# Delta units that cross between halves of the array, attention heads in pairs, layers written out

## The chip, the cores and the metric

The kernel runs on one core of a Trainium2 chip. The core has TensorE (PE, matrix products from SBUF into PSUM), VectorE (DVE), ScalarE (ACT), GpSimd (POOL) and SyncE (SP, which issues most transfers), each with its own in-order queue of instructions, coupled by semaphores. The metric is the device time of one execution in microseconds; lower is better. The profile and all its rows come from one profiled execution.

## What is computed

The reference has two parts that follow each other on one sequence of 256 tokens with 1,024 channels, in f32. Cut to what this change touches:

```python
def first_block(x, c, ctx, ...):             # one layer
    z_x, z_c = split(norm(x) @ w_in), split(norm(ctx) @ w_in)
    ya = rwkv_mixer(z_c, z_x, ...)           # 8 heads of 64, both directions, 512 tokens
    yb = na_mixer(z_c, z_x, ...)             # 8 heads of 64, 256 queries, 512 keys
    x = x + gate * branch_merge(ya, yb)
    return x + gate * moe(norm(x))

# rwkv_mixer, one step of the scan, per head and direction (s is 64x64):
s = s * w_t - (s @ kk_t) (kk_t * a_t)^T + v_t k_t^T ;  y = s @ r_t

# na_mixer, per head:
q = rms_norm(q) * q_g * 64 ** -0.5 ; k = rms_norm(k) * k_g
p = softmax([q @ k_x^T + bias (masked to a window), q @ k_c^T]) ; y = p @ [v_x; v_c]

# second part: two layers (each: four mixers, merge, then 8 heads x 16 looked-up experts a token)
for l in range(2):
    x = layer(x, weights[l])
```

## The kernel before

`build` runs `first_block` and then `second_block`. Every stage is a block of its own that ends with a barrier of all engines, and no work is begun across one.

`first_block`: the input products (`linear`), `head_scales` (the norms of the heads, which also multiplies q by the gain `q_g`), `na_attention`, `delta`, `close`, `moe`. `second_block` (L3485) is a loop on the chip, `Fori(0, 2)`, over `layer`, which runs `mixers` and `merge_peer`; the layer's number is a register, from which SP computes the addresses of the weights. In `merge_peer` each token's 128 experts are gathered row by row.

`na_attention` (L1376) works on units, a head and one half of the queries (128 queries x 512 keys, of which the first 256 are context), 16 in all. Per unit: PE multiplies scores (L1416; a head's 64 channels lie on one half of the partitions), DVE scales the context half (L1468), scales the other half and adds the masked bias (L1470), takes the maximum of 512 columns (L1473) and negates it (L1474), ACT takes the exponential and the sum (L1450), DVE the reciprocal (L1486) and the division of all 512 columns (L1487), PE transposes (L1439), ACT copies (L1459), PE mixes with v into 64 output rows (L146), DVE copies out (L1480). PE's order puts the scores of unit n+2 ahead of the transposes of unit n. GpSimd adds the mask to the bias (L1406).

`delta` (L561) does the scan in 4 steps of 128 tokens, both directions (d) at once, by chunks of 64 tokens: 16 units of a head and a direction, each with two chunks, one on either half of the partitions (`half(c)`). A triangular system is inverted by squaring: the matrix P and its transpose lie in `MP[:, u, 0:2]`, the sum so far in `MP[:, u, 2]`. In round s of 0 to 5 (`SQ` is 5) PE squares P (L739), multiplies the transpose and, from round 1, the sum (L743, L746), for 8 groups of two units; ACT copies the powers back (L889, 128x256, 128x128 in round 4), DVE adds the product to the sum (L1029, 128x128), after ACT. All products here go from half c to half c, so two of the four 64x64 quadrants of PE are in use, in turn. Behind round 0 PE has the products with V (L696) and the turning of tokens (L711), which waits for DVE's tails (L982, L983), behind round 1 the decays' logs of the next step (L644). DVE has the tails, the blends of the next step (L934 to L939), then the sums, and behind rounds 2 and 3 the operands of the next step (L950 to L965). ACT copies the turned tokens between rounds 0 and 1 (L903 to L906), and behind round 1 the exponentials of the next step (L871). After round 5 come the solution (L763), the factor (L771: the one product here whose four quadrants alternate, two of them into each bank), the state's additions and its advance. The other order of things is set by the code as written, engine by engine.

## Time and profile before

| | us |
|---|---|
| median of 3 runs | 2974.51 (2971.76 to 2982.3) |
| the profiled execution: its time | 2983.61 |
| its span, first to last instruction | 2981.8 |
| `na_attention` (238.8 to 291.7) | 52.9 |
| `delta` (292.2 to 553.1) | 260.9 |
| layer 0 of `second_block` (1035.6 to 2004.1) | 968.5 |
| layer 1 (2004.2 to 2976.9) | 972.7 |

A row of the timeline has the start, the duration, the engine, the line, the operation, output and inputs, the partitions x columns and the count; in brackets stands the idle time before it and who ended it. "issue" is idle time that nothing in the profile explains. PE's products in f32 stand in the trace as two instructions each, its transposes as one; L644's 8 products of a step, for instance, are x16. PEld is the load of weights. A window's row has the busy time of PE, PEld, DVE, ACT and POOL with their counts, then PEclk, the granted clock of PE as a share of 2.4 GHz (0.5 is its lower level, 1.2 GHz), and the transfers' share and rate.

### The profile page before, as it was taken

Reading aid. Unit: us, or ns where it says so; the run is one execution under the profiler, and the core shown is the slowest. Engines: PE = TensorE matmul, PEld = TensorE weight load, DVE = VectorE, ACT = ScalarE, POOL = GpSimd, SP = SyncE. Lnnn points to the kernel's source line nnn. Section 1 sums busy time; section 2 is a strip of 40 time slices with the busy share of each in tenths; the row PEclk is TensorE's granted clock in tenths of the full one; section 3 lists DMA queues with packets and bytes.
Section 4 is the critical chain, followed back from the end, with each engine's and each line's share of the span. In section 5 each row is a group of like instructions: output and inputs, shape, how many; then the busy total and the mean of one; then the engine's idle time right before and its main releaser. Section 6 shows DMA issues by size and latency. Waiting matters only on the chain. (4 is left out here: it accounts for less than half of the span.)

```text
span 2981.8 us, 44173 instructions
## 1 busy us (share of the span) xinstructions
PE 2631.6 (88%) x17318; PEld 1869.5 (63%) x17318; DVE 1994.0 (67%) x4159; ACT 1177.4 (39%) x2270; POOL 656.9 (22%) x570
## 2 busy tenths in 40 slices
PE   7999888889999799999997787879999999887877
PEld 5895788778888689985553333338998555333333
DVE  5546665559999656567767777645665777677764
ACT  4243554348888544522222222234552322213222
POOL 0001000000004100004444454420000444454442
PEclk9999999989999899999999999989999999899998
DMA  7640000339999443359999999974345999999997
GB/s 311 235 187 24 3 3 3 121 127 351 371 379 371 166 161 128 142 200 417 421 417 422 422 421 421 421 315 163 117 152 198 395 421 418 422 421 421 421 422 320
DMA packets 121060, 838.88 MB, mean 281 GB/s; under 512 B 15402, under 2 KB 18380, under 8 KB 19732
## 3 DMA queue, kind: packets, MB, share of 16 engines
q0 software_dynamic: 77600, 564.43, 45.8%
q1 hardware_dynamic: 43252, 271.59, 24.2%
q8 instruction: 141, 2.31, 0.3%
q14 instruction: 67, 0.55, 0.1%
HBM read 834.65 MB, written 1.05 MB: 280 GB/s over the span
## 5 line engine op out<-in xcount | busy, mean ns | idle before, releaser
L3087 PE MATMUL bank<-uv_rows,z_o 128*128 128x512 f32 x872 | 435.1, 645 | 85.1 <-ACT z_o L3215 85.0
L3087 PEld LDWEIGHTS bank<-uv_rows,z_o 128*128 128x128 f32 x872 | 176.0, 206 | 320.1 <-issue 209.5
L3430 DVE CUSTOM_DVE_ANT_0 uv_rows<-uv_rows,ring 128x1024 f32<-128x1024 f32 x218 | 265.6, 1224 | 162.6 <-DMA uv_rows<-in_peer_uv,peer_index 162.2
L2967 POOL DMA_INDIRECT uv_rows<-in_peer_uv,peer_index x218 | 251.8, 1155 | 411.5 <-PE bank L3087 253.4
L3087 PE MATMUL bank<-z_mg,z_o 128*128 128x512 f32 x528 | 259.9, 638 | 55.4 <-ACT z_o L3215 55.3
L1805 DVE TENSOR_TENSOR moe_halves<-ring,moe_halves 128x1024 fp32r<-128x1024 f32 x240 | 285.6, 1221 | 29.7 <-ACT moe_halves L1729 27.4
L3087 PE MATMUL bank<-query_weights,z_o 128*128 128x512 f32 x544 | 256.7, 619 | 55.1 <-ACT z_o L3215 55.1
L3209 ACT ACTIVATE peer_gelu<-peer_act 128x4 f32<-128x4 f32 (+2 forms) x134 | 27.5, 205 | 703.2 <-DVE peer_act L3430 703.2
L3215 ACT ACTIVATE z_o<-square,peer_wts 128x128 f32<-128x128 f32 x512 | 164.4, 390 | 257.1 <-DVE peer_wts L3444 240.1
L1729 ACT ACTIVATE moe_halves<-ring 128x1024 fp32r<-128x1024 f32 x240 | 249.0, 1059 | 42.7 <-PE bank L161 42.4
L2630 DVE TENSOR_TENSOR x_weights<-ring,x_weights 128x1024 fp32r<-128x1024 f32 x116 | 140.7, 1224 | 156.9 <-ACT x_weights L2470 156.4
L159 PE MATMUL bank<-x_halves,x_weights 128*128 128x256 f32 x800 | 233.5, 292 | 2.5 <-DVE x_nk L2639 2.5
L3430 DVE CUSTOM_DVE_ANT_0 query_weights<-query_weights,ring 128x1024 f32<-128x1024 f32 x136 | 165.2, 1225 | 93.1 <-DMA query_weights<-in_peer_uv,peer_index 93.1
L3087 PEld LDWEIGHTS bank<-query_weights,z_o 128*128 128x128 f32 x544 | 104.1, 196 | 196.2 <-issue 119.9
L3087 PEld LDWEIGHTS bank<-z_mg,z_o 128*128 128x128 f32 x528 | 105.3, 205 | 193.1 <-issue 122.5
L160 PE MATMUL bank<-x_halves,x_weights 128*128 128x256 f32 x800 | 226.3, 283 | 0.0
L161 PE MATMUL bank<-x_halves,x_weights 128*128 128x256 f32 x800 | 226.1, 283 | 0.0
L3430 DVE CUSTOM_DVE_ANT_0 z_mg<-z_mg,ring 128x1024 f32<-128x1024 f32 x132 | 160.8, 1224 | 91.4 <-DMA z_mg<-in_peer_uv,peer_index 91.4
L2967 POOL DMA_INDIRECT z_mg<-in_peer_uv,peer_index x132 | 158.9, 1203 | 190.0 <-PE bank L3087 174.6
L2967 POOL DMA_INDIRECT query_weights<-in_peer_uv,peer_index x136 | 157.0, 1154 | 158.0 <-PE bank L3087 141.8
L2470 ACT ACTIVATE x_weights<-ring 128x1024 fp32r<-128x1024 f32 x116 | 121.9, 1056 | 174.6 <-PE bank L161 174.6
L159 PEld LDWEIGHTS bank<-x_halves,x_weights 128*128 128x128 f32 x800 | 153.1, 191 | 10.0 <-issue 6.3
(644 smaller groups left out, 5729.6 us busy)
## 6 DMA issues: line engine op xcount, KB each, us to landing
ring<-in_moe SPq DMA_DIRECT2D x96, 1024.0 KB, 6.9
ring<-in_w_in SPq DMA_DIRECT2D x83, 1024.0 KB, 5.0
ring<-in_mod_rows SPq DMA_DIRECT2D x16, 1024.0 KB, 4.8
ring<-in_w_out SPq DMA_DIRECT2D x12, 1024.0 KB, 6.8
ring<-in_mod_w SPq DMA_DIRECT2D x8, 1024.0 KB, 11.9
ring<-in_w_branch SPq DMA_DIRECT2D x8, 1024.0 KB, 8.8
query_weights<-in_peer_wq SPq DMA_DIRECT2D x8, 1024.0 KB, 9.9
ring<-in_peer_wq SPq DMA_DIRECT2D x6, 1024.0 KB, 6.5
```

Source lines behind the costliest of these rows:

```text
L159: pe.matmul(out, a[0], b[0], start=first, stop=False)
L160: pe.matmul(out, a[0], b[1], start=False, stop=False)
L161: return pe.matmul(out, a[1], b[0], start=False, stop=last)
L1729: act.activation(w2[:, p % 4, 0, :], C.ring[:, n % RING, COLUMNS[c]], ACT.Copy)\
L1805: dve.tensor_tensor(w2[:, p % 4, 1, :], C.ring[:, n % RING, COLUMNS[c]], w2[:, p % 4, 0, :].bitcast(F32), ALU.subtract).then_inc(S["low"], 1)
L2470: act.activation(w2[:, p % 4, 0, :], C.ring[:, n % TS, COLUMNS[c]], ACT.Copy).then_inc(S["high"], 1)
L2630: dve.tensor_tensor(w2[:, p % 4, 1, :], C.ring[:, n % TS, COLUMNS[c]], w2[:, p % 4, 0, :].bitcast(F32), ALU.subtract).then_inc(S["low"], 1)
L2967: pool.indirect_dma_start(out=row(j), out_offset=None, in_=A["peer_uv"], in_offset=bass.IndirectOffsetOnAxis(ap=index[:, g, k:k + 1], axis ...
L3087: ins = pe.matmul(bank[2 * t + c][:, :], diag[:, q % 2, i, :], row(j)[:, D + c * 512:D + (c + 1) * 512], start=(j % (PH * TOPK) == 0), sto ...
L3209: act.activation(gel[:, q % 2, 0:size], acts[:, g % 2, c:c + size], ACT.Gelu).then_inc(S["gelu"], 1)
L3215: ins = act.activation(diag[:, q % 2, n, :], C.sq["ident"], ACT.Copy, scale=wts[:, q % 2, n:n + 1])
L3430: dve.tensor_tensor_reduce(u, u, xtok[:, t, :], 1.0, 0.0, ALU.mult, ALU.add, acts[:, g % 2, j % TOPK:j % TOPK + 1]).then_inc(S["dots"], 1)
```

## The change

In `delta`, a unit's place changes from round to round: `lies(i, s, c)` tells on which half chunk c of unit i lies in round s. The first unit of a pair stays on its half; the second goes over to the other half in rounds 1, 2, 3 and 4, there and back, so that the products of rounds 1 to 4 use all four quadrants; rounds 0 and 5 use two. The products are issued for two groups at a time (`square_round`), as 64x64 products, by kind, then by unit, then by chunk; a bank holds the first or the second units of two groups (a batch). The sum is written otherwise: `MP` has four parts, P, its transpose, P plus the identity (2) and the product so far (3). DVE no longer adds to the sum in SBUF: `advance_sums` writes, out of PSUM and with a mask of identity and zero, parts 2 and 3 in one addition (128x256; in rounds 0 and 4 only part 2, 128x128; in round 5 a copy). Round 0 now has such additions too. ACT takes the batches in the order 0, 1, 2, DVE in the order 1, 0, 3, 2, each waiting so that they are not in the same bank. From round 2 on eight banks are used in place of four. `MP` is larger, `ZT` moves into `ya`.

In `na_attention`, a pair is two heads, one on either half of the partitions. The scaling by 64 ** -0.5 goes into `q_g` in `head_scales`. The bias has a context half of zeros, cleared by GpSimd; one `tensor_tensor_reduce` adds it and takes the maximum of 512 columns. The division goes: DVE makes a diagonal of reciprocals, and PE multiplies with it where it transposed (a product, so two instructions for one). The mixes of the two heads alternate between halves of the output rows. Scores of pair m+2 now stand behind the turning of pair m.

In `second_block` the loop is a Python loop: the layers stand one behind the other in the program, with fixed addresses.

```diff
+                dve.tensor_scalar(C.v["q_g"], C.v["q_g"], HD ** -0.5, None, ALU.mult).then_inc(S["q_gain"], 1)
...
+    rbank = lambda s, b: bank[b % 4 if s < 2 else b]
+    batch = lambda b: slice(2 * groups[b - b % 2][1] + groups[b][0] * NH + b % 2,
+                            2 * groups[b - b % 2][1] + groups[b][0] * NH + b % 2 + 3, 2)
+    def lies(i, s, c):
+        return c ^ (i & (s - 1) & 1) if s else c
...
+                def emptied(s, b):
+                    if s < 2 and b >= 4:
+                        taken(s, b - 4)
+                    elif s == 1 or s == 2 and b < 4:
+                        taken(s - 1, b + 4)
+                    elif s == 2:
+                        pe.wait_ge(S["tok"], len(turns))
+                        pe.wait_ge(S["w_out"], 2)
+                        if not last:
+                            pe.wait_ge(stages[step + 1]["decays"], 4)
+                def square_round(s, k):
+                    powers = ([(1, 0, 0)] if s < SQ else []) + ([(0, 1, 1)] if s < SQ - 1 else []) + \
+                             ([(2, 3, 2)] if s else [])
+                    for q in range(2):
+                        for left, right, at in powers:
+                            for i in range(2):
+                                u = groups[2 * k + q][0] * NH + 2 * groups[2 * k + q][1] + i
+                                out = rbank(s, 2 * k + i)[:, q * 192 + at * CH:q * 192 + (at + 1) * CH]
+                                for c in range(CC):
+                                    h, to = half(lies(i, s, c)), half(lies(i, min(s + 1, SQ), c))
+                                    part = lambda n: X[h, u, 0, :] if s == 0 and n == 1 else MP[h, u, n, :]
+                                    ins = pe.matmul(out[to], part(left), part(right), start=True, stop=True)
+                    ins.then_inc(S["round"], 1)
                 for s in range(SQ + 1):
-                    for g, (d, p) in enumerate(groups):
...
-                                    ins = pe.matmul(out[r, 2 * CH:3 * CH], m, MP[r, u, 2, :], start=True, stop=True)
-                        ins.then_inc(S["round"], 1)
+                            taken(s - 1, 2 * k + 1)
+                        emptied(s, 2 * k + 1)
+                        square_round(s, k)
...
+                    to, of = (slice(0, 2), slice(0, 2)) if s < SQ - 1 else (slice(3, 4), slice(2, 3))
+                    for b in range(NG):
+                        act.wait_ge(S["round"], s * (NG // 2) + b // 2 + 1)
+                        if b % 2:
+                            act.wait_ge(S["summed"], s * NG + b)
+                        act.activation(MP[:, batch(b), to, :], rbank(s, b)[:, 0:384]
+                                       .rearrange("p (u a t) -> p u a t", u=2, a=3)[:, :, of, :], ACT.Copy)\
+                           .then_inc(S["power"], 1)
                     if s == 1 and not last:
                         decays(step + 1)
                     if s == 0:
...
                                       units(X, d)[:, :, 0, :], ALU.subtract).then_inc(S["start"], 1)
+                def advance_sums(s, b):
+                    dve.wait_ge(S["round"], s * (NG // 2) + b // 2 + 1)
+                    if s < SQ and b % 2 == 0:
+                        dve.wait_ge(S["power"], s * NG + b + 1)
+                    of = rbank(s, b)[:, 0:384].rearrange("p (u a t) -> p u a t", u=2, a=3)
+                    if s == SQ:
+                        ins = dve.tensor_copy(MP[:, batch(b), 3, :], of[:, :, 2, :])
+                    elif s in (0, SQ - 1):
+                        ins = dve.tensor_tensor(MP[:, batch(b), 2, :], of[:, :, 0, :],
+                                                C.masks[:, 4, :].unsqueeze(1).broadcast_to([P, 2, CH]), ALU.add)
+                    else:
+                        ins = dve.tensor_tensor(MP[:, batch(b), 2:4, :], of[:, :, 0:3:2, :],
+                                                C.masks[:, 4:6, :].unsqueeze(1).broadcast_to([P, 2, 2, CH]), ALU.add)
+                    ins.then_inc(S["summed"], 1)
+                for b in range(NG):
+                    advance_sums(0, b ^ 1)
...
+                        advance_sums(s, b ^ 1)
                     if s in (2, 3) and not last:
                         operands(step + 1, s - 2)
                 dve.wait_ge(S["factor"], 1)
...
+                    sp.wait_ge(S["biased"], n - 3)
...
+                pool.memset(bias[:, :, 0:CTX], 0.0).then_inc(S["cleared"], 1)
...
+                def scores(m):
+                    if m >= 2:
+                        pe.wait_ge(S["biased"], 2 * m - 2)
+                    for n in (2 * m, 2 * m + 1):
+                        h, t = units[n]
+                        ins = pe.matmul(C.bank[n % 4][:, :], qn[part(n), h // 2, cut(t)], kn[part(n), h // 2, :],
+                                        start=True, stop=True)
+                    ins.then_inc(S["scores"], 1)
+                def turn(m):
+                    pe.wait_ge(S["inverted"], 2 * m + 2)
+                    S.wait(pe, "turned_out", 2 * m)
+                    for n in (2 * m, 2 * m + 1):
+                        for k in range(4):
+                            ins = pe.matmul(C.bank[4 + n % 2][:, cut(k)], sc[:, n % 4, cut(k)], diag[:, n % 4, :],
+                                            start=True, stop=True)
+                        ins.then_inc(S["turned"], 1)
+                def mix(m):
+                    pe.wait_ge(S["turned_out"], 2 * m + 2)
+                    S.wait(pe, "out", m - 1)
+                    for k in range(4):
+                        for n in (2 * m, 2 * m + 1):
+                            h = units[n][0]
+                            ins = pe.matmul(C.bank[6 + m % 2][part(n), 0:P], Z["vb"][:, k, h * HD:(h + 1) * HD],
+                                            pT[:, n % 4, cut(k)], start=(k == 0), stop=(k == 3))
+                    ins.then_inc(S["mixed"], 1)
...
+                for m in range(M):
+                    turn(m)
+                    if m + 2 < M:
+                        scores(m + 2)
+                    if m:
+                        mix(m - 1)
+                mix(M - 1)
...
+                for m in range(M):
+                    if m + 1 < M:
+                        exp(m + 1)
+                    S.wait(act, "mixed", m - 1)
...
+                def begin(m):
+                    dve.wait_ge(S["scores"], m + 1)
+                    S.wait(dve, "turned", 2 * m - 2)
+                    for n in (2 * m, 2 * m + 1):
+                        dve.wait_ge(S["bias_masked"], n + 1)
+                        dve.tensor_tensor_reduce(sc[:, n % 4, :], C.bank[n % 4][:, :], bias[:, n % 4, :], 1.0, NEG, ALU.add,
+                                                 ALU.max, mx[:, n:n + 1]).then_inc(S["biased"], 1)
+                    dve.wait_ge(S["biased"], 2 * m + 2)
+                    dve.tensor_scalar(low[:, 2 * m:2 * m + 2], mx[:, 2 * m:2 * m + 2], -1.0, None, ALU.mult)\
+                       .then_inc(S["lowered"], 1)
...
+                dve.wait_ge(S["cleared"], 1)
...
+                for m in range(M):
+                    dve.wait_ge(S["exp"], 2 * m + 2)
+                    S.link(dve, dve.reciprocal(rs[:, 2 * m:2 * m + 2], rs[:, 2 * m:2 * m + 2]), "inverse")
+                    for n in (2 * m, 2 * m + 1):
+                        dve.tensor_scalar(diag[:, n % 4, :], C.sq["ident"], rs[:, n:n + 1], None, ALU.mult)\
+                           .then_inc(S["inverted"], 1)
+                    if m + 2 < M:
+                        begin(m + 2)
+                    if m:
+                        take(m - 1)
+                take(M - 1)
...
-    with C.nc.Fori(0, 2) as l_:
+    for l_ in range(2):
         layer(C, A, l_, xT)
```

What each engine's queue holds at three places:

PE in `na_attention`, before, from its first instruction (L1416 scores, L1439 transposes, L146 mix).

```order
1245 L1409 UNCONDITIONAL_BRANCH
1246 L1416 MATMUL bank<-z_kb,z_q 128x512 x3
1247 L1439 MATMUL bank<-square,na_scores 128x128 x4
1248 L1416 MATMUL bank<-z_kb,z_q 128x512
1249 L1439 MATMUL bank<-square,na_scores 128x128 x4
1250 L146 MATMUL bank<-na_probsT,z_vb 64x128 x4
```

The same place after (L1451 scores, L1460 the product with the diagonal, L1470 mix).

```order
1245 L1444 UNCONDITIONAL_BRANCH
1246 L1451 MATMUL bank<-z_kb,z_q 128x512 x4
1247 L1460 MATMUL bank<-na_inverse,na_scores 128x128 x8
1248 L1451 MATMUL bank<-z_kb,z_q 128x512 x2
1249 L1460 MATMUL bank<-na_inverse,na_scores 128x128 x8
1250 L1451 MATMUL bank<-z_kb,z_q 128x512 x2
1251 L1470 MATMUL bank<-na_probsT,z_vb 64x128 x8
```

The scores moved from ahead of a unit's transposes to behind a pair's turning.

DVE in the first step of `delta`, before, from the start of the sum (L1003) to round 3: tails, copies, blends, sums (L1029), operands.

```order
293 L1003 TENSOR_TENSOR b_mp<-masks,ring 128x8x64
294 L982 TENSOR_TENSOR z_q<-z_kb,b_ein 128x4x128
295 L983 TENSOR_TENSOR b_eneg<-z_kb,b_ein 128x512
296 L982 TENSOR_TENSOR z_q<-z_kb,b_ein 128x4x128
297 L983 TENSOR_TENSOR b_eneg<-z_kb,b_ein 128x512
298 L1009 COPY ring<-bank 128x8x64 x2
...
306 L1029 TENSOR_TENSOR b_mp<-b_mp,bank 128x2x64 x16
307 L950 COPY b_qr<-ring 128x4x2
308 L951 TENSOR_TENSOR b_qr<-ring,b_ein 128x4x2x63
309 L960 TENSOR_TENSOR z_kb<-z_kb,b_eneg 128x512
310 L965 TENSOR_TENSOR z_kb<-z_kb,b_eneg 128x512
311 L1029 TENSOR_TENSOR b_mp<-b_mp,bank 128x2x64 x8
```

The same place after (L1021 is the start, L1032 and L1035 are `advance_sums`).

```order
247 L1021 TENSOR_TENSOR b_mp<-masks,ring 128x8x64
248 L1032 TENSOR_TENSOR b_mp<-bank,masks 128x2x64 x8
249 L1000 TENSOR_TENSOR z_q<-z_kb,b_ein 128x4x128
250 L1001 TENSOR_TENSOR b_eneg<-z_kb,b_ein 128x512
...
261 L1035 TENSOR_TENSOR b_mp<-bank,masks 128x2x128 x16
262 L968 COPY b_qr<-ring 128x4x2
263 L969 TENSOR_TENSOR b_qr<-ring,b_ein 128x4x2x63
264 L978 TENSOR_TENSOR z_kb<-z_kb,b_eneg 128x512
265 L983 TENSOR_TENSOR z_kb<-z_kb,b_eneg 128x512
266 L1035 TENSOR_TENSOR b_mp<-bank,masks 128x2x128 x8
```

Eight additions of round 0 came in ahead of the tails, and those of rounds 1 to 3 are twice as wide.

PE at the end of a layer, before: the last rows of the loop's body, then the branch back.

```order
6520 L3076 MATMUL bank<-square,ring 128x128 x8
6521 L2922 UNCONDITIONAL_BRANCH
6522 L3486 REGISTER_ALU
6523 L3486 COMPARE_AND_BRANCH
```

The same place after, layer 0 and the begin of layer 1.

```order
5287 L3117 MATMUL bank<-square,ring 128x128 x8
5288 L2963 UNCONDITIONAL_BRANCH
5289 L2295 UNCONDITIONAL_BRANCH
5290 L153 MATMUL bank<-square 128x512 x4
5291 L159 MATMUL bank<-x_halves,x_weights 128x256
```

The register's step and the compared branch are gone; the jump out of one block and into the next stands there as between all other stages.

## Rows read from the trace of the kernel before

**Rows 1.** The page's first part: busy time of each engine.
```profile
PE 2631.6 (88%) x17318; PEld 1869.5 (63%) x17318; DVE 1994.0 (67%) x4159; ACT 1177.4 (39%) x2270; POOL 656.9 (22%) x570
```

**Rows 2.** Windows: attention, then each delta step from round 0 to L763.
```profile
238.80:291.70 52.90, 48.99 (x224) 28.52 (x224) 38.78 (x112) 23.77 (x49) 11.54 (x16) 0.87 0.11 33
310.34:349.12 38.78, 35.29 (x825) 33.92 (x827) 24.46 (x72) 25.22 (x67) 0.00 (x0) 1.00 0.01 3
369.11:410.48 41.37, 36.70 (x824) 35.46 (x825) 25.73 (x74) 25.22 (x67) 1.03 (x1) 0.96 0.01 3
432.57:472.55 39.98, 35.29 (x824) 33.92 (x826) 25.67 (x73) 24.78 (x66) 0.00 (x0) 1.00 0.01 3
497.38:530.81 33.43, 32.41 (x793) 31.85 (x795) 16.76 (x52) 19.14 (x52) 0.00 (x0) 0.95 0.01 3
```

**Rows 3.** Windows of 5 us in attention, for the granted clock.
```profile
250.00:255.00 5.00, 5.00 (x15) 2.78 (x14) 2.34 (x7) 1.41 (x3) 0.72 (x1) 0.50 0.10 26
...
260.00:265.00 5.00, 4.86 (x28) 3.12 (x28) 4.56 (x13) 2.46 (x5) 0.73 (x1) 1.00 0.16 47
```

**Rows 4.** Timeline of attention at the full clock.
```profile
265.07 0.49 DVE L1487 TENSOR_SCALAR na_scores<-na_scores,na_sum 128x512 f32<-128x512 f32 x1
...
265.62 0.66 PE L1439 MATMUL bank<-square,na_scores 128*128 128x128 f32 x4
...
266.20 1.09 PE L146 MATMUL bank<-na_probsT,z_vb 128*64 128x128 f32 x8
...
266.43 0.69 DVE L1473 TENSOR_REDUCE na_max<-na_scores 128x1 f32<-128x512 f32 x1
...
268.27 0.66 PE L1439 MATMUL bank<-square,na_scores 128*128 128x128 f32 x4
...
273.06 0.16 DVE L1486 RECIPROCAL na_sum<-na_sum 128x1 f32<-128x1 f32 x1
...
273.80 0.66 PE L1439 MATMUL bank<-square,na_scores 128*128 128x128 f32 x4
...
276.54 0.66 PE L1439 MATMUL bank<-square,na_scores 128*128 128x128 f32 x4
```

**Rows 5.** Nearest rows for what is new: the page's group L3430, and timeline rows.
```profile
L3430 DVE CUSTOM_DVE_ANT_0 uv_rows<-uv_rows,ring 128x1024 f32<-128x1024 f32 x218 | 265.6, 1224 | 162.6 <-DMA uv_rows<-in_peer_uv,peer_index 162.2
```
```profile
308.32 1.14 PE L146 MATMUL bank<-lora_w,z_lw 64*128 64x512 f32 x4
...
327.94 2.05 PE L644 MATMUL bank<-square,w_sig 128*128 128x128 f32 x16
```

**Rows 6.** Delta: a group by line, and timeline rows of the first step.
```profile
L1029 DVE TENSOR_TENSOR b_mp<-b_mp,bank 128x128 f32<-128x128 f32 x160 | 41.5, 285 | 47.3 <-ACT b_mp L889 40.3 <-PE bank L746 3.7 <-PE bank L743 2.9
```
```profile
305.85 1.56 DVE L991 TENSOR_TENSOR ring<-bank,masks 128x256 f32<-128x256 f32 x4
...
331.67 0.97 ACT L889 ACTIVATE b_mp<-bank 128x256 f32<-128x256 f32 x3
...
353.49 1.16 PE L771 MATMUL bank<-b_btok,ring 64*64 64x64 f32 x64 [0.69 <-ACT ring L910]
```

**Rows 7.** Delta: waits of PE and the end of ACT's token copies; a window's clock.
```profile
325.09 0.34 PE L739 MATMUL bank<-b_mp 64*64 64x64 f32 x4 [1.49 <-DVE b_mp L1029]
...
404.96 0.30 PE L739 MATMUL bank<-b_mp 64*64 64x64 f32 x2 [2.00 <-DVE b_mp L1029]
...
510.47 1.21 ACT L889 ACTIVATE b_mp<-bank 128x256 f32<-128x256 f32 x4
```
```profile
405.00:410.00 5.00, 5.00 (x113) 5.00 (x115) 2.44 (x11) 1.11 (x4) 0.60 (x1) 0.66 0.01 3
```

**Rows 8.** The edge between layers: PE's branch, its first products, the mixers' barrier.
```profile
L3486 PEldq COMPARE_BRANCH  x1: 3468/3468/3468, 2004.3 to 2004.3; - x1
```
```profile
1035.77 5.37 PE L153 MATMUL bank<-square 128*128 128x512 f32 x8 [3.41 <-PEq L73]
...
2007.88 6.43 PE L153 MATMUL bank<-square 128*128 128x512 f32 x8 [6.61 <-issue]
```
```profile
L2224 PEldq EVENT_SEMAPHORE  x2: 51/51/51, 1272.0 to 2245.2; - x2
```

197 lines of the change are left out of this document (56 added, 141 removed).

## Prediction

> **What bounds the kernel now.** I read the page first, then the windows by stage, then the timeline of the three places that the change touches. The span is 2981.8 us, of which the two layers with the gathers take from 1035.8 to 2976.9. TensorE (PE) is busy 88% of the span [rows 1], but that share says nothing about a stage, so each stage is read by what ends its waits. No transfer runs in the windows attention and no prefetched work crosses the barriers there, so what these two stages give is handed on one for one to everything behind them.
>
> Attention lasts 52.9 us at a mean granted clock of 0.87 [rows 2]. Between 250 and 255 us the clock is at its half level, 1.2 GHz, and back at 2.4 GHz from 260 [rows 3]; a mean of 0.87 over 52.9 us is 13.8 us at half. At the full level a head's half (a unit) takes 2.65 to 2.74 us (the starts of L1439 in [rows 4]), 5.4 a pair, and VectorE (DVE) is nearly full with it.
>
> The delta stage has four steps. From round 0 to L763 a step takes 38.8, 41.4, 40.0 and 33.4 us [rows 2]. There the rounds of squarings stream on PE: half a round, four groups, runs from 325.09 to L644 at 327.94, 2.85 us with its tail [rows 7], so 5.4 us a round. In the last step PE is busy 32.4 of 33.4 us; in the first three 3.5 to 4.7 us are idle, ended by DVE [rows 2, 7].
>
> At the edge between the layers the trace shows one branch of 3,468 ns on PE, and the first matmul 3.6 us after it began, against a first layer in which it starts as soon as the barrier is past [rows 8].
>
> **Layers written out.** Layer 0's mixers run 1035.77 to 1272.0, 236.2 us. Layer 1's run from the branch at 2004.3 to 2245.2, 240.9 us [rows 8]. The difference of 4.7 is the branch and what follows it (first matmuls at half clock), less the 0.2 which the first layer also needs behind its barrier. No taken branch back is left in the order of the new program. I take **4.5 us** off, with 3.5 (the branch alone) and 4.7 as ends, and zero as a rival, since the new code of layer 1 still begins with a jump into its block. The register arithmetic for addresses sits on SP's queue, which waits for DVE's L2630 and so hides it.
>
> **Attention in pairs.** Work for a pair falls on every engine. PE, where a product in f32 is two instructions in the trace and a transpose is one: 16 instructions of 128 columns for the turning product with the diagonal in place of 8 transposes, at (2.05-0.28)/15 = 0.118 us (L644) [rows 5], 1.9 us; two scores on different row halves, for which the row of four 512-column instructions in 1.14 us stands [rows 5], so 1.1; the mix, 16 instructions, alternating column halves, 8 of them took 1.09 [rows 4], so 1.0. DVE: two reductions fused with the bias addition; 128x1024 took 1,224 ns (L3430) [rows 5], and a 512-column reduction 0.69 (L1473) [rows 4], so 0.60 and 0.69; reciprocal 0.16; two diagonals of 128 columns between 0.16 and 0.49 (L1486, L1487) [rows 4], taken 0.28; negation 0.15 and one copy of 0.3. DVE's work for a pair falls from 5.2 to 2.6 us. If DVE were a throughput limit, PE's 4.0 would become the bound and 11 us would go.
>
> But the order speaks against that. The scores of pair m+2 stand behind the turning of pair m on PE, and DVE's start of m+2 stands ahead of its diagonals of m+1. So the steps of one pair are in series: reciprocal and two diagonals 0.74, semaphore 0.07, turning 1.84, scores 1.15, begin 1.45, copy 0.3: **5.55 us a pair**, no less than the 5.4 of now. Only the mix, ScalarE (ACT) and the other pair's exponentials are covered. The gain is in the ends: the first reciprocal comes 5.3 us after the start (the clearing of the bias's 1,024 context columns on GpSimd, one more step before it, included, between 0 and 2 us and taken 1), six pairs have a later pair to begin, 33.3, and the last two need 7.6 because nothing is begun in them. That is 46.2 us at full clock. At half clock turning and scores double and a pair takes 8.5, so 13.8 us at half would cost 4.8 and give 51.0. PE idles 3.9 us before its first turning, so I expect a half-clock stretch again, but turnings with more work in it; I take 49.9, a gain of **3 us**, ends 0 and 7.
>
> **Delta units across the halves.** Rounds 1 to 3 have 96 products of 64 columns, 192 instructions, spread over four quadrants in the alternation that L771 has, where 64 instructions took 1.16 us, 15 ns each [rows 6]. A round is 2.9 us of PE in place of 5.4; round 4 is 1.9 in place of 3.7; rounds 0 and 5 stay on two quadrants and keep their time. The new bound is DVE: every batch of two units is one addition of 128x256 out of PSUM, 0.39 us in a row of four (L991) [rows 6], against 285 ns for 128x128 (L1029) of now [rows 6]. I take 0.40, so 3.2 us a round; 0.48, with a full start and a semaphore each time, is the upper end, 3.8. ACT's copies (0.97 for three) alternate with it on the other bank and stay below that.
> The walk through the first step: ACT can't take round 2 until its exponentials end at 331.67 [rows 6], 21.3 us after the step's round 0, as now, because the token copies, the blends and the table loads ahead of it don't change. The eight additions of round 0, new on DVE, delay its tails by 3 us, into its idle stretch before L1009; about 0.3 us comes out of it. From 331.67: copy 0.4, seven additions 2.8, operands of the next step 2.1 (three DVE operations of 0.69), round 3 3.2, operands 2.1, round 4 2.3, the first copies of round 5 0.5: 345.1 against L763 at 349.1, so 4.0 gained. In steps 1 and 2 the operands are 2.7 each, the sum is 21.3+14.6 = 35.9, against 41.4 and 40.0: 5.5 and 4.1. In the last step nothing is put between, and the wait is ACT's tokens to 510.47 [rows 7], 13.1 us in, 0.4 later through the additions of round 0; then 3.7, 3.3, 3.3, 2.3 and 0.5: 26.6 against 33.4, 6.8. Sum **20.4 us** at the full clock; at 0.48 a batch 14.
>
> The clock takes some of it back. In the second step PE's 2.00 us wait before 404.96 is followed by five microseconds with a mean granted clock of 0.66, which is 3.4 us at the half level [rows 7]. In the new order PE waits 3.8 us in round 1 (banks of ACT and DVE before groups 5 to 8) and 2.2 us before round 5, in each step. Such a stretch costs up to 1.7 where PE is the limit (logs, round 5, L763), and nothing where DVE is. I take 1.5 us a step, **6 us**, between 0 and 14. Delta's net is 14.4.
>
> A rule to weigh here. L771's quadrants with rows 0 to 63 and with rows 64 to 127 write the same bank at 15 ns an instruction [rows 6]. The Trainium skill, TensorEngine Tiling (Array Packing), section Gotcha 1: PSUM Pressure, says that different row tiles cannot access the same PSUM bank simultaneously. By that rule the products would come in two turns, 29 ns each, a round would be 5.6 us as now, and the delta gain would be nothing; L771 shows it not to hold for this pattern, in which the two write different partitions.
>
> **The sum.** 4.5 + 3 + 14.4 = 21.9 us. On the profiled execution's own 2983.6 us it gives 2961.7; that execution is 9.1 above the median of the runs, 2974.5, and the stages that change have no part that varies from run to run, so I carry the difference over: 2952.6, forecast **2953 us**.
>
> **Rivals.**
> 1. *The clock takes more.* With PE idle 40% of a step, two stretches at half fall in each, and additions are late at 0.48. Delta gives 5, attention 1, layers 4.5: 10.5 us, 2964. For it: [rows 3], 13.8 us at half with PE never idle in them. Against it: the delta steps now recover within 4 us [rows 7].
> 2. *Everything at full clock.* Delta 20, attention 6.7, layers 4.7: 31 us, 2943. Against it: the idle gaps that the walk contains.
> 3. *Slower.* If the half level (1.2 GHz) holds through a step as it does in attention, rounds 1 to 4 take 5.6 us each for 192 instructions, as long as now, and rounds 0 and 5, the logs and L763 double: 3.7+1.9+2+3.7 = 11 us more a step, of which some 3 fall into waits. Four steps of 8, less 4.5 for the layers: 2974.5+32-4.5 = 3002. It decides once more than half of a step is at the half level; now it is at most a tenth (a mean of 0.95 in the last step).
> 4. *The written-out layers bring nothing*, as a jump at layer 1's begin still waits for code: 4.5 less, 2957. It lies in the forecast's range.
>
> **How the numbers follow.** Forecast 0.60 (its own range 2946 to 2962, rival 4 within it at 0.12), rival 1 0.22, rival 2 0.12, rival 3 0.04, rest 0.02. Within 0.3%, which is 8.9 us and about what a measurement of this kernel can tell from no change, lie savings under 8.9, a fifth of rival 1 and the rest: 0.06. Slower 0.04, faster 0.90. The range takes in rivals 1 and 2 but for their outer parts: 2942 to 2965.
>
> **What would show it.** Right: attention's period is 5.5 us a pair, with PE's wait for DVE's diagonals ahead of the turning and DVE's wait for scores; in rounds 2 and 3 the waits of PE are ended by DVE's additions, these lie 0.40 us apart, and a four-quadrant instruction takes 15 ns; the step ends 4 to 7 us earlier; layer 1's mixers last as long as layer 0's. Wrong: attention at 4 us a pair (the chain has slack I missed), rounds of 5 us (the quadrants don't run together), additions further apart than 0.5 us, a branch or an issue gap of 3 us between the layers, or a granted clock below 0.8 in the delta windows.

## The result, and the profile after

| | us |
|---|---|
| before, median of 12 runs | 2977.99 (2971.76 to 2987.19) |
| after, median of 12 runs | 2967.84 (2959.55 to 2972.36) |
| ratio | 0.9962, 95% interval 0.995 to 0.9975 |
| the profiled execution after: time, span | 2972.05, 2970.3 |
| forecast | 2953, range 2942 to 2965 |

The change is faster by 10 us (7 to 15), where 21.9 had been forecast. Profile against profile it is 11.5 us. The busy time of PE fell, as [rows 1] can be set against, while its count of instructions rose by 832; the row `q8 instruction` further down the page gets its meaning in the experiments.

```profile
PE 2589.2 (87%) x18150; PEld 1840.3 (62%) x18150; DVE 1993.1 (67%) x4152; ACT 1174.6 (40%) x2270; POOL 654.9 (22%) x571
...
q8 instruction: 144, 2.36, 0.3%
```

The stages, from barrier to barrier, in us:

| stage | before | after | difference |
|---|---|---|---|
| input products | 217.3 | 221.7 | +4.4 |
| head norms | 21.5 | 21.6 | +0.1 |
| attention | 53.9 | 51.9 | -2.0 |
| delta | 260.4 | 254.0 | -6.4 |
| close | 73.6 | 74.6 | +1.0 |
| moe | 408.8 | 409.9 | +1.1 |
| mixers, layer 0 | 238.0 | 235.8 | -2.2 |
| rest of layer 0 | 730.6 | 726.6 | -4.0 |
| mixers, layer 1 | 242.6 | 238.7 | -3.9 |
| rest of layer 1, to the span's end | 735.1 | 735.5 | +0.4 |

Input products, close, moe and the rests are not touched by the change. Over the profiles of this study the input products took 215.3 to 221.7 and the rest of layer 0 725.7 to 730.6, so their differences are what varies from run to run. The mixers of layer 0 do the same work in both kernels, and differ by 2.2. The three places that changed give 12.3 together.

Each stage's time comes from one profiled execution of its kernel, and a stage with the same code can differ from one such execution to the next: the attention of before takes 53.9 us here and 50.0 in a later experiment (Layers alone), its delta 260.4 and 261.8; the delta of after takes 254.0 here and 251.7 in another.

Windows of after: attention, delta, then its four steps from round 0 to the solution (L780, before L763). They answer to [rows 2]; the columns are the same.

```profile
243.30:295.20 51.90, 36.01 (x288) 26.84 (x288) 19.24 (x72) 22.99 (x49) 12.34 (x17) 0.93 0.11 32
295.20:549.20 254.00, 188.44 (x6656) 173.46 (x6656) 169.13 (x417) 128.17 (x320) 2.08 (x2) 0.94 0.01 4
314.00:351.17 37.17, 27.97 (x1019) 26.32 (x1018) 27.89 (x75) 24.57 (x67) 0.00 (x0) 0.95 0.01 4
371.01:410.04 39.03, 29.14 (x1016) 27.53 (x1017) 30.48 (x81) 24.67 (x67) 1.03 (x1) 0.93 0.01 4
431.49:468.50 37.01, 28.17 (x1017) 26.50 (x1019) 29.80 (x79) 23.93 (x66) 0.00 (x0) 0.95 0.02 4
494.52:526.97 32.45, 24.40 (x985) 22.81 (x986) 21.19 (x59) 18.50 (x52) 0.00 (x0) 0.95 0.02 5
```

Read the first number behind each window against [rows 2]: 38.8, 41.4, 40.0 and 33.4 have become 37.2, 39.0, 37.0 and 32.5, 7.9 us in place of the 20.4 of the walk. The stage as a whole gained 6.4: 1.5 were lost outside these windows, 1.2 of them ahead of the first step. PE is busy 28 of 37 us, so it is not PE's work that fills a step any more. The granted clock of the stage is 0.94; the same window of before has 0.97.

Where PE's time goes stands in its timeline. First the middle of the first step, rounds 2 to 5 (L753), then the last step from the second half of round 1 on, where DVE has no operands to make between the rounds:

```profile
337.16 1.41 PE L753 MATMUL bank<-b_mp 64*64 64x64 f32 x81 [0.90 <-ACT b_eneg L888]
339.38 2.09 PE L753 MATMUL bank<-b_mp 64*64 64x64 f32 x127 [0.81 <-issue]
342.97 2.17 PE L753 MATMUL bank<-b_mp 64*64 64x64 f32 x126 [1.50 <-issue]
346.80 1.44 PE L753 MATMUL bank<-b_mp 64*64 64x64 f32 x82 [1.65 <-issue]
```
```profile
508.65 7.76 PE L753 MATMUL bank<-b_mp 64*64 64x64 f32 x369 [2.16 <-ACT b_mp L906]
517.83 2.09 PE L753 MATMUL bank<-b_mp 64*64 64x64 f32 x127 [1.42 <-issue]
521.43 2.31 PE L753 MATMUL bank<-b_mp 64*64 64x64 f32 x126 [1.51 <-issue]
525.42 1.74 PE L753 MATMUL bank<-b_mp 64*64 64x64 f32 x50 [1.68 <-issue]
```

The crossing itself does nearly what was forecast: 127 instructions in 2.09 us are 16.5 ns each, with 15 forecast, against 28 on two quadrants. But PE then stands still, mostly for 1.4 to 1.8 us, "issue": nothing that the row names was missing. Neither DVE nor ACT ends these waits. Once they have begun they come after 126 or 127 instructions, whatever round is going on, and end 3.6 to 4.0 us apart. Behind a wait with another cause PE runs on longer: in the last step 369 instructions without one such wait, 21 ns each, behind 2.16 us of waiting for ACT. No such wait stands in the squarings of before. The page has one more row that counts in such pieces: queue `q8 instruction` moved 144 packets and 2.36 MB, 16.4 KB each. 127 products' instructions stand beside as many weight loads; with a few waits on semaphores that is about 256 instructions. And 144 times 256 is 36,864, where PE has 18,150 products and as many loads, 36,300, in the whole program. So the first theory, from here on **A**: PE has used up its instructions and waits for the next block of them.

The same execution shows the packets of this queue one by one. From 335 to 351 us there are four; in a row of 40 slices, 0.4 us each, a slice with 41 GB/s is one packet of 16.4 KB:

```profile
GB/s 0 0 0 0 41 0 0 0 0 0 0 0 0 0 41 0 0 0 0 0 0 0 41 20 0 0 0 0 0 0 20 0 41 0 0 0 0 0 0 0
q8 instruction: 4, 0.07, 1.6%
```

They begin at 336.6, 340.6, 343.8 and 347.8, to within a slice. 1.6% of 16 engines over 16 us are 1.0 us a packet. The three waits without a cause end at 339.38, 342.97 and 346.80, each 2 to 3 us after one of the first three packets began. Behind the fourth PE has no such wait; DVE holds it there for 0.66 us.

Two more places of the same profile. In the middle of round 1, PE waits for DVE, and the clock falls behind it:

```profile
329.85 2.84 PE L753 MATMUL bank<-b_mp 64*64 64x64 f32 x96 [3.54 <-DVE b_mp L1035]
```
```profile
330.00:335.00 5.00, 5.00 (x138) 4.76 (x140) 2.09 (x5) 3.12 (x7) 0.00 (x0) 0.74 0.01 3
```

96 instructions that take 1.64 at the full clock take 2.84. That is theory **C**, the clock. Theory **B** is that DVE's additions bound the rounds. They are as fast as forecast: four of them, 128x256, in 1.42 us, 0.355 each:

```profile
344.12 1.42 DVE L1035 TENSOR_TENSOR b_mp<-bank,masks 128x256 f32<-128x256 f32 x4 [0.19 <-ACT b_mp L906]
```

Attention at the full clock, one pair and the begin of the next (L1524 the reciprocal, L1526 the diagonals, L1460 the turning, L1451 the scores, L1508 the start). It answers to [rows 4].

```profile
263.33 0.16 DVE L1524 RECIPROCAL na_sum<-na_sum 128x2 f32<-128x2 f32 x1
263.52 0.48 DVE L1526 TENSOR_SCALAR na_inverse<-square,na_sum 128x128 f32<-128x128 f32 x2
264.06 2.05 PE L1460 MATMUL bank<-na_inverse,na_scores 128*128 128x128 f32 x16 [1.38 <-DVE na_inverse L1526]
266.05 1.13 PE L1451 MATMUL bank<-z_kb,z_q 64*128 64x512 f32 x4
267.10 1.09 PE L1470 MATMUL bank<-na_probsT,z_vb 128*64 128x128 f32 x16
267.22 0.69 DVE L1508 CUSTOM_DVE_ANT_0 na_scores<-bank,na_bias 128x512 f32<-128x512 f32 x1 [3.21 <-PE bank L1451]
...
268.84 0.16 DVE L1524 RECIPROCAL na_sum<-na_sum 128x2 f32<-128x2 f32 x1
```

From reciprocal to reciprocal 5.51 us, with 5.55 forecast, and the steps of the series have the lengths that they were given, within 0.15 us.

At the edge of the layers the branch is gone, and PE starts with the barrier (1996.1), but at half clock as before (6.4 us for 8 instructions; [rows 8] has 6.43, and layer 0 of after has 3.67).

```profile
1996.22 6.42 PE L153 MATMUL bank<-square 128*128 128x512 f32 x8 [2.94 <-PEq L73]
```

### The profile page after: what moved, and what is told of

Read it like the earlier page. It is cut to its first block and busy times, and to the rows that moved or that the text cites. A ratio compares the mean times of both kernels' runs of the same rounds, so it can differ in the third digit from the quotient of the medians.

```text
span 2970.3 us, 45520 instructions
## 1 busy us (share of the span) xinstructions
PE 2589.2 (87%) x18150; PEld 1840.3 (62%) x18150; DVE 1993.1 (67%) x4152; ACT 1174.6 (40%) x2270; POOL 654.9 (22%) x571
## 3 DMA queue, kind: packets, MB, share of 16 engines
q8 instruction: 144, 2.36, 0.3%
```

## The experiments

"Delta" is the stage from barrier to barrier, each from the one profiled execution of its kernel. The same delta code differed by up to 5.9 us from one such execution to another (248.2 and 242.3, below), so a difference of that size between two kernels shows nothing by itself. The ratios of whole times are given beside.

### Two quadrants again

```diff
     def lies(i, s, c):
-        return c ^ (i & (s - 1) & 1) if s else c
+        return c
```

> The changed kernel with lies() returning c: every product of the squarings stays on its own half, so two of the four quadrants are in use, as before the change. Banks, batches, number of instructions and all additions and copies stay. Three theories. (A) PE's instructions arrive too slowly. In the changed kernel PE runs 126 or 127 instructions of products (as many weight loads stand beside them) and then waits 1.4 to 1.8 us for nothing that the profile names, over and over; 576 product instructions from round 2 to L780 take 15.3 to 16.6 us, 27 to 29 ns each, as much as on two quadrants before. By A the crossing brings almost nothing: with two quadrants an instruction takes 28 ns, the gaps without a cause shrink or vanish, and round 2 to L780 lasts 16 to 17 us; the whole of delta moves by less than 3 us from 254.0. (B) The additions of DVE and their turns with ACT bound the rounds. Then PE's doubled time of 28 ns (5.4 us for 192) becomes the bound over the 4.0 to 4.6 of now, and each step is 3 to 5 us longer, delta 266 to 274. (C) The half clock is what took the gain: PE, busier now, idles less, the stretches at half clock in delta fall from 27 us to those of the kernel before, 17, and delta changes by the balance of B and some 5 us less.

Measured: 2973.52, ratio to before 0.9976 (0.996 to 0.9992). Delta, and PE's row of the first step behind the logs:

```profile
290.90:552.80 261.90, 221.33 (x6656) 208.82 (x6656) 170.33 (x417) 130.17 (x320) 2.08 (x2) 0.96 0.02 4
```
```profile
330.20 17.59 PE L753 MATMUL bank<-b_mp 64*64 64x64 f32 x576
```

The waits without a cause are gone from rounds 1 to 5: 576 instructions in one row, without one gap. That was A's sign, and the first three steps take 17.4 to 18.7 us from round 2 to the solution, where A had 16 to 17. But delta is 7.9 us longer, and A had said under 3, B 12 to 20. So the crossing is worth about 7.9 us in the changed kernel, and neither theory alone gives that. Only 4.5 of it lie between round 2 and the solution, summed over the four steps. The whole times show less of it: 0.9976 against 0.9962, 4 us, and the two intervals overlap.

### Narrow additions

```diff
-                        ins = dve.tensor_tensor(MP[:, batch(b), 2:4, :], of[:, :, 0:3:2, :],
-                                                C.masks[:, 4:6, :].unsqueeze(1).broadcast_to([P, 2, 2, CH]), ALU.add)
+                        ins = dve.tensor_tensor(MP[:, batch(b), 2, :], of[:, :, 0, :],
+                                                C.masks[:, 4, :].unsqueeze(1).broadcast_to([P, 2, CH]), ALU.add)
```

> The changed kernel, in which DVE's additions of rounds 1 to 3 write only part 2 (128x128 in place of 128x256); the sum (part 3) is left out, so the output is not the reference's. An addition falls from 355 to 460 ns to 290. (A) Instructions arrive too slowly: nothing changes from round 2 to L780, 15.3 to 16.6 us a step, delta stays within 2 us of 254.0, since DVE's additions already wait for PE. (B) Additions bound the rounds: 24 additions a step, 0.1 us less each, 2.4 us a step, delta 244 to 246.

One execution, 2965.47. The kernel leaves out the sum (part 3).

```profile
288.60:542.60 254.00, 189.52 (x6656) 175.15 (x6656) 157.65 (x417) 128.26 (x320) 2.08 (x2) 0.93 0.02 4
```

DVE's busy time falls by 11.5 us, from 169.1 to 157.7, and delta is 254.0, to the tenth what it was, where B had 244 to 246. The mean clock is 0.93 in place of 0.94, which may hide a microsecond or two, not eight. B falls as far as the width of the additions goes: that is not what bounds the changed kernel.

### Fewer instructions for the same squarings

```diff
-                    powers = ([(1, 0, 0)] if s < SQ else []) + ([(0, 1, 1)] if s < SQ - 1 else []) + \
-                             ([(2, 3, 2)] if s else [])
+                    powers = ([(1, 0, 0, 1), (0, 1, 1, 1)] if s == 0 else [(2, 1, 0, 1), (1, 2, 1, 2)] if s < SQ - 1 else
+                              [(2, 1, 0, 1), (1, 3, 2, 1)] if s < SQ else [(1, 3, 2, 1)])
...
-                    for b in range(NG):
+                    for b in range(NG if s else 0):
                         act.wait_ge(S["round"], s * (NG // 2) + b // 2 + 1)
...
+                    elif s == 0:
+                        ins = dve.tensor_tensor(MP[:, batch(b), 1:3, :], of[:, :, 0:2, :],
+                                                IM[:, 0:2, :].unsqueeze(1).broadcast_to([P, 2, 2, CH]), ALU.add)
                     else:
-                        ins = dve.tensor_tensor(MP[:, batch(b), 2:4, :], of[:, :, 0:3:2, :],
-                                                C.masks[:, 4:6, :].unsqueeze(1).broadcast_to([P, 2, 2, CH]), ALU.add)
+                        ins = dve.tensor_tensor(MP[:, batch(b), 1:4:2, :], of[:, :, 0:3:2, :],
+                                                IM[:, 2:4, :].unsqueeze(1).broadcast_to([P, 2, 2, CH]), ALU.add)
```

(`IM` holds I, -I, 2I and 0; the fourth number of a product is its width in parts of 64 columns.)

> The changed kernel with the squarings written so that a round needs two products a unit and chunk in place of three, for the same result. With A the triangular matrix, B = A - I is kept in place of the transpose, and only P + I of the other: (P - I)(P + I) = P^2 - I, to which DVE adds 2I, and one product 128 columns wide gives (I + A)[A - I, S] = [A^2 - I, S']. So rounds 1 to 3 have 128 instructions of products in place of 192 (the columns stay 192 a unit and chunk), DVE's additions are as wide as now, but in round 0 (128x256 in place of 128x128), ACT copies 128 columns in place of 256 in rounds 1 to 3 and nothing in round 0. (A) Instructions arrive too slowly: rounds 2 and 3 have a third fewer of them, 3.7 us each in place of 5.4, with rounds 4 and 5 as before; round 2 to L780 falls by 3 us, and another 1 to 1.5 in round 1 where PE catches up: delta 254.0 less 12 to 18, so 236 to 242, the whole kernel 0.4 to 0.6% faster than the changed one. (B) DVE's additions bound the rounds: they are as many and as wide; only ACT's shorter copies free the banks sooner: 0 to 1.5 us a step, delta 248 to 254. (C) The clock: PE has less work and idles more, so more time at half clock; no gain.

Measured: 2958.14, ratio to before 0.9914 (0.9881 to 0.9947).

```profile
290.50:538.70 248.20, 189.94 (x5888) 173.18 (x5888) 171.03 (x421) 105.13 (x288) 2.08 (x2) 0.92 0.01 3
```

5.8 us off delta, where A had said 12 to 18; 248.2 lies at the edge of B's range, 248 to 254, which it gave for ACT's shorter copies. So this run alone does not decide between them; the split product below does. The count of `q8` fits A: 768 products' instructions and 768 weight loads fewer are 1,536, or 6 times 256, and the page of this kernel has 138 packets where the changed kernel has 144. The waits without a cause in the squarings fall from 17.5 us over the four steps to 5.9. The clock is lower, 0.92, which C had said; what that hides shows below, where the same delta runs with another clock.

The 2,816 product instructions of the squarings that are left are as many as the kernel before had. There the transpose and the sum shared a left side in rounds 1 to 3, one product of 128 columns:

```profile
L743 PE MATMUL bank<-b_mp 64*64 64x128 f32 x768 | 65.8, 270 | 0.0
```

The change had split it in two, and so made 3,584 instructions of the 2,816: in rounds 1 to 3 it asked PE for half as many again, and wanted them in half the time.

### Attention: scores and diagonals ahead

```diff
                 for m in range(M):
-                    turn(m)
                     if m + 2 < M:
                         scores(m + 2)
+                    turn(m)
...
+                invert(0)
                 for m in range(M):
-                    dve.wait_ge(S["exp"], 2 * m + 2)
...
+                    if m + 1 < M:
+                        invert(m + 1)
                     if m + 2 < M:
                         begin(m + 2)
```

(`invert` is the reciprocal and the two diagonals.)

> The changed kernel with two lines of attention's order moved: on PE the scores of pair m+2 stand ahead of the turning of pair m, and on DVE the reciprocal and the two diagonals of pair m+1 stand ahead of the start of pair m+2. The theory of the chain: of the period of 5.51 us a pair (all seven steps of it in series: reciprocal and diagonals 0.74, turning 1.9, scores 1.13, start 1.45) scores and diagonals leave the chain. What is left is PE's own work, turning 1.9, scores 1.1, mix 1.05: 4.1 us a pair at the full clock. Four periods are at full clock, so 4 x 1.4, two at half clock give 0.7 to 1.5 each: attention 51.9 (barrier to barrier) less 7, so 43.5 to 46.5. Rival: another chain stands right behind, start of m+2, its two exponentials 1.42, diagonals, turning, which closes over two pairs: (1.45+1.42+0.8+1.9)/2 = 2.8 us, below PE's work; so if the period stays above 4.6 us it is something I do not see, for instance the clock, which falls when PE waits.

Measured: 2950.9, ratio to before 0.9898 (0.9864 to 0.9932). Attention and delta, and PE's order:

```profile
237.00:274.40 37.40, 32.46 (x288) 24.32 (x288) 20.68 (x72) 21.62 (x49) 12.27 (x17) 1.00 0.16 44
274.40:526.10 251.70, 185.90 (x6656) 170.99 (x6656) 168.94 (x417) 128.08 (x320) 2.08 (x2) 0.96 0.02 4
```
```profile
253.39 1.13 PE L1451 MATMUL bank<-z_kb,z_q 64*128 64x512 f32 x4
254.45 2.05 PE L1460 MATMUL bank<-na_inverse,na_scores 128*128 128x128 f32 x16
256.43 1.09 PE L1470 MATMUL bank<-na_probsT,z_vb 128*64 128x128 f32 x16
257.45 1.13 PE L1451 MATMUL bank<-z_kb,z_q 64*128 64x512 f32 x4
```

4.06 us from scores to scores, the sum of PE's three parts, as expected. The stage is 14.5 us shorter, twice what was expected. From the first turning to the seventh it takes 22.4 us in place of 36.1. The changed kernel spends 7.48 and 7.11 us on its first two periods, reciprocal to reciprocal, in place of 5.51: the half clock costs it 3.6, and here the granted clock is 1.00 throughout in place of 0.93. The other 10 are the shorter chain. In the changed kernel PE stands still for 4.67 us ahead of its first turning and is at half level behind; here the scores of pair 2 stand in that wait, and waits of 1.24 and 1.79 are left of it. That this is why the clock stayed up was not tested by itself.

### PE kept busy in round 1

```diff
                         emptied(s, 2 * k + 1)
...
+                        if s == 1 and k == 2:
+                            pe.wait_ge(S["tok"], 3)
+                            for j in range(12):
+                                pe.matmul(bank[6][:, 0:P], C.sq["ident"], C.sq["ones"], start=True, stop=True)
```

> The changed kernel with 12 products of 128 columns (identity times ones, into a part of PSUM that nothing reads) put on PE in the middle of round 1, where PE waits 3.54 us in each of the first three steps for the additions behind DVE's blends; they take 24 x 0.118 = 2.8 us at the full clock and end before the wait does. Theory of the clock: the wait is followed by a stretch at the half clock in every step (means of 0.74, 0.73 and 0.79 over the five microseconds behind it in the first three steps), in which the second half of round 1 takes 2.8 us in place of 1.6 and the logs up to 3.5 in place of 2.05. With PE kept busy that stretch stays away, the exponentials end 21.3 to 21.8 us after the step's round 0 in place of 22.2 to 23.0, and delta falls from 254.0 by 4 to 6. Rival: the clock falls all the same (the wait is not what it follows), and delta stays within 1.5 us of 254.0, or grows by as much as the products outlast the wait.

One execution, 2965.88. Delta, and the place in the first step:

```profile
292.80:547.30 254.50, 196.06 (x6752) 180.34 (x6752) 169.35 (x417) 128.26 (x320) 2.07 (x2) 0.96 0.01 4
```
```profile
323.87 2.94 PE L766 MATMUL bank<-square 128*128 128x128 f32 x24
327.27 1.82 PE L753 MATMUL bank<-b_mp 64*64 64x64 f32 x96 [0.46 <-ACT b_mp L910]
329.02 2.05 PE L653 MATMUL bank<-square,w_sig 128*128 128x128 f32 x16
```

The clock's part came as expected: no half level behind the wait, the logs take 2.05, the exponentials end 21.8 after round 0 in all three steps (23.0, 22.8 and 22.2 in the changed kernel). The gain did not: delta is 254.5. What the exponentials win, up to 1.2 us, is lost again behind them; in the first step round 2 to the solution takes 17.8 against 16.6, with 4.0 us of waits without a cause. The step is 37.2 long, as in the changed kernel. A explains it: moving work earlier does not help a queue that is short of instructions. The 96 added products' instructions make it one block longer (145 packets).

### Layers alone

The kernel before, with `for l_ in range(2)` in place of the loop on the chip, and each layer's buffers named apart; nothing else.

> The kernel before with the third part of the change alone: the two layers written out. By the trace of the changed kernel the branch and the 3.6 us behind it are gone, but PE's first products of the second layer still run at half clock (6.42 us as before). So the second layer's mixers go from 242.6 to 238.5 to 239, and the whole saves 3.5 to 4, 0.13%, which three rounds can hardly tell from nothing; every other stage as in the kernel before. Rival: the longer program costs something elsewhere (addresses, code loading in the gathers' stage), and the two layers together save less than 2.

Measured: 2976.90 against 2976.63, ratio 0.9999 (0.9986 to 1.0012). The mixers of its two layers:

```profile
1035.00:1271.10 236.10, 227.48 (x1898) 209.83 (x1898) 138.64 (x222) 123.07 (x205) 1.70 (x3) 1.00 0.42 146
2000.50:2239.20 238.70, 231.57 (x1898) 212.02 (x1898) 138.62 (x222) 123.10 (x205) 1.70 (x3) 0.98 0.41 144
```

The second layer's mixers take 238.7 again, as in the changed kernel, 3.9 less than before. In the time of the whole nothing of it is seen; 3.9 us is 0.13%, just inside the interval. So the branch's time is gone where it stood, and whether the whole is shorter by it stays open.

This run also gives a second execution of the old attention, whose code it has unchanged:

```profile
241.00:291.00 50.00, 45.37 (x224) 26.58 (x224) 38.89 (x112) 23.78 (x49) 11.54 (x16) 0.93 0.12 35
```

It takes 50.0 us at a mean clock of 0.93, where the profile of before has 53.9 at 0.87. The attention of the changed kernel takes 51.7 to 52.3 in the five profiles that have it.

### Both gains together

The diffs of the third and the fourth experiment in one kernel.

> The changed kernel with both edits that gained alone: fewer instructions in the squarings (delta 248.2 in place of 254.0) and attention's scores and diagonals ahead (37.4 in place of 51.8). They are in different stages with a barrier between, so their gains add: 5.8 + 14.4 = 20.2 us off the changed kernel, 2947 to 2949 where the changed kernel has 2967.8; ratio to the kernel before 0.986 to 0.990. Against it only where the clock's stretches at half fall: up to 3 us either way.

Measured: 2941.95, ratio to before 0.9879 (0.986 to 0.9898).

```profile
239.50:277.80 38.30, 32.53 (x288) 24.31 (x288) 21.70 (x72) 21.61 (x49) 12.34 (x17) 1.00 0.15 43
277.80:520.10 242.30, 183.44 (x5888) 166.37 (x5888) 170.53 (x421) 104.66 (x288) 2.08 (x2) 0.96 0.01 3
```

More than the sum. Delta is the very code of the third experiment, and takes 242.3 in place of 248.2: the means of the clock, 0.96 and 0.92, are some 19 and 40 us at the half level. The stage began at another moment, and the run was on another chip; of what the profiles show, the clock is what differs. If all of it is the clock's, 20 us more at half cost this stage 5.9, about 0.3 us each. The delta of the changed kernel (254.0 at 0.94) and the same code in the fourth experiment (251.7 at 0.96) give much the same: 10 us more at half, 2.3 us. By that rate, an estimate, the changed kernel's 0.94 against 0.97 before, some 15 us more at half, cost some 4 us.

### Round 1 moved up, whole and in half

```diff
-                    for d in range(2):
-                        blend(step + 1, d)
+                    blend(step + 1, 0)
...
                         advance_sums(s, b ^ 1)
+                    if s == 1 and not last:
+                        blend(step + 1, 1)
...
                             ins.then_inc(S["tok"], 1)
+                            if n in (3, 4):
+                                for b in range(2 * n - 6, 2 * n - 4):
+                                    back(1, b)
```

(`back` is ACT's copy of a batch.)

> The last kernel, with the work of round 1 moved up on two queues: ACT's copies of round 1's first four batches stand behind the fourth and the fifth copy of turned tokens instead of behind all six, and DVE's second blend of the next step stands behind round 1's additions in place of ahead. In the changed kernel and in the one with fewer instructions PE waits 3.3 to 3.5 us in the middle of round 1 for exactly these, then runs at half clock. Expected if round 1 is the limit up to the exponentials: that wait falls below 1.2 us, the stretch at half clock goes with it, the exponentials end 2 to 4 us earlier after round 0, in three steps, and some 2 us in the last: delta 248.2 less 6 to 13. Rival: something else of the first part (the tokens, the table loads, the logs) holds the exponentials, or the second blend, now behind, holds round 2's additions: then the wait only moves, delta within 2 us of 248.

Measured: 2938.22, ratio to before 0.9862 (0.9843 to 0.9881), the lowest ratio of the study, though its interval overlaps that of the kernel with both gains.

```profile
279.00:520.80 241.80, 186.12 (x5888) 168.80 (x5888) 170.21 (x421) 103.57 (x288) 2.08 (x2) 0.95 0.01 3
```
```profile
310.22 0.90 PE L754 MATMUL bank<-b_mp 64*64 64x64 f32 x32 [0.98 <-ACT b_mp L907]
```

PE's wait in round 1 fell from 3.3 to 0.98 and the exponentials end 20.1 after round 0, as expected, and 241.8 lies in the range given, 248.2 less 6 to 13. But the kernel with both gains has 242.3 without this edit, and against that the stage wins 0.5 us: round 2 to the solution takes 16.4 to 17.7 in the first three steps, where it took 15.0 to 17.2. The half with the copies alone:

> The kernel of e7 with only ACT's half of what e8 moved: round 1's first four copies stand between those of the turned tokens, while both blends of DVE stay ahead of round 1's additions. In e8 the exponentials ended 20.1 us after round 0 in place of 21.3 to 22.5, but round 2 to the solution took 16.4 to 17.7 in place of 15.0 to 17.2, which I put to the blend that now stands behind round 1. If so, here DVE's blends (they end 14.7 us after round 0) set the wait in round 1, the exponentials end at 21.0 to 21.5, round 2 goes at its old speed, and delta is 241 to 243, no better than either: DVE's queue is the limit of the first part. If it is the copies on ACT that held it, delta is 237 to 240.

Measured: 2941.3, ratio 0.9865 (0.9843 to 0.9887).

```profile
279.60:523.90 244.30, 186.83 (x5888) 169.12 (x5888) 170.42 (x421) 104.03 (x288) 2.08 (x2) 0.94 0.01 3
```

The exponentials end at 22.5 to 22.8 here and delta is 244.3, both a little later than expected (21.0 to 21.5, 241 to 243), so the copies alone bring nothing, as expected if DVE's blends hold round 1. In the first step of the kernel with both gains DVE works from 319.23 to the solution with hardly a gap, additions and operands in turn. So with fewer instructions the order on DVE is the likely bound of the middle of a step, which is what the prediction had taken for the changed kernel. No run shortened that queue, so this is argued, not shown.

### The split product, and two quadrants with few instructions

```diff
-                    powers = ([(1, 0, 0, 1), (0, 1, 1, 1)] if s == 0 else [(2, 1, 0, 1), (1, 2, 1, 2)] if s < SQ - 1 else
+                    powers = ([(1, 0, 0, 1), (0, 1, 1, 1)] if s == 0 else [(2, 1, 0, 1), (1, 2, 1, 1), (1, 3, 2, 1)] if s < SQ - 1 else
```

> The kernel of e7 with one thing put back: the product of 128 columns in rounds 1 to 3, (I + A)[A - I, S], is again two of 64 columns. Columns, algebra, additions, copies and banks are the same; PE has 192 instructions of products a round in place of 128. (A) Instructions arrive too slowly: waits of 1.4 to 1.9 us without a cause come back, three or four a step, and delta goes from 242.3 to 250 to 253 (e4, the same attention with the squarings of the changed kernel, had 251.7). (B) What gained in e3 was ACT's copies, half as wide and none in round 0: delta stays 242 to 244. (C) The columns count: no difference either, since they are the same.

Measured: 2949.64, ratio 0.9891 (0.9867 to 0.9914).

```profile
277.70:531.80 254.10, 188.33 (x6656) 173.89 (x6656) 170.90 (x421) 106.41 (x288) 2.08 (x2) 0.94 0.01 4
```
```profile
317.46 2.92 PE L754 MATMUL bank<-b_mp 64*64 64x64 f32 x180
321.79 2.10 PE L754 MATMUL bank<-b_mp 64*64 64x64 f32 x127 [1.41 <-issue]
325.38 2.08 PE L754 MATMUL bank<-b_mp 64*64 64x64 f32 x126 [1.49 <-issue]
328.99 1.39 PE L754 MATMUL bank<-b_mp 64*64 64x64 f32 x79 [1.52 <-issue]
```

This is the cleanest of the tests of A. Columns, additions and copies are those of the kernel with both gains; only one product has become two. The waits are back behind 126 and 127 instructions, their ends 3.6 us apart, and the page has 144 packets again for 138. Delta is 254.1 in place of 242.3, 11.8 longer (of which, by 0.94 against 0.96, some 3 may be the clock's). The whole time bears it out on one chip: 2946.7 to 2952.1 over four executions, where the kernel with the early copies alone has 2940.2 to 2945.3, 8 us less at the median, with a delta 9.8 shorter.

And the kernel with both gains, with the one-line diff of the first experiment (`lies()` returns c):

> The kernel of e7 with lies() returning c, so that all its products stay on two quadrants. With 128 instructions a round their supply is no limit (3.7 us), and PE's time is: 28 ns for 64 columns and 55 for 128, 5.3 us a round against 2.9 with the crossing. If the crossing brings what my prediction gave it once the instructions keep up, rounds 2 and 3 are 1.5 to 2 us longer each, a step 4 to 6, delta 242.3 plus 14 to 22: 256 to 264, near the 260.4 of the kernel before. If the crossing brings little even then, because DVE's chain bounds the step, delta is 244 to 250. In the changed kernel (e1) taking the crossing away cost 7.9.

Measured: 2948.03, ratio 0.9893 (0.987 to 0.9916).

```profile
274.70:526.30 251.60, 215.16 (x5888) 201.62 (x5888) 172.04 (x421) 107.69 (x288) 2.08 (x2) 0.97 0.01 3
```
```profile
312.75 17.00 PE L754 MATMUL bank<-b_mp 64*64 64x64 f32 x448
```

9.3 us longer than with the crossing: below the 14 to 22 of the one expectation, and 1.6 above the range of the other, in which DVE's chain bounds the step. PE streams, as before the change. So with few instructions the crossing is worth 9.3 and with many 7.9. PE's busy time falls by 32 and 33 us; where the rest of that goes was not tested, and DVE's chain is the likely place.

One thing stays open. The two kernels on two quadrants, 261.9 with many instructions and 251.6 with few, differ by 10.3 as well, though neither shows a wait without a cause in rounds 2 to 5. They differ in ACT's copies too, and no run separates the two there.

## Why the prediction was wrong

**Layers, forecast 4.5.** The mixers of layer 1 lost 3.9: the branch of 3.5 and the latency behind it. What had made 4.7 of it, half clock in the first products, stayed. The term is 0.6 too large by this stage, and the whole kernel with this part alone could not show it (0.9999). The size is uncertain by more than that: in two other profiles with the layers written out (two quadrants, and PE kept busy) the first products took 5.1 us and these mixers 235.9, 6.7 less than before.

**Attention, forecast 3, measured 2.0, and that by luck.** The chain is right to 0.04 us a pair: 5.51 against 5.55, all in series, DVE's work halved and nothing gained by it in the middle. The experiment that took scores and diagonals out of the chain gave PE's 4.06 at once. One term was mis-sized: the end behind the seventh reciprocal, from 285.37 to the last copy's end at 294.45, is 9.1 and not 7.6, since two mixes and the last turning follow each other on PE. The half clock cost 3.6, and the forecast's 49.9 held 3.7 for it. What the forecast didn't see is that its starting point was a bad one: the 52.9 of before had a mean clock of 0.87, and the same code took 50.0 from barrier to barrier at 0.93. Against that execution the new attention, 51.9 at 0.93, is 1.9 slower. So the gain in this term is the clock of the profile of before, and whether the edit of attention gained anything is not shown.

**Delta, forecast 14.4 net, measured 6.4.** Here the prediction failed, and in one step of it: "The new bound is DVE". The sum went "A round is 2.9 us of PE in place of 5.4", from 15 ns an instruction, a rate read in a burst of 64 [rows 6]. The rate holds (16.5 ns over 127). What does not hold is that PE can keep it up: a round has 192 products' instructions and as many weight loads, one and a half blocks of 256, and in the rows with the waits a block comes every 3.6 to 4.0 us. That is 5.4 us or more a round, by supply, as long as on two quadrants. In the trace the 576 instructions from round 2 on take 16.0 to 18.1 us a step up to the solution, 28 to 31 ns each. The waits of the profile before never showed it, because there a round of 5.4 us had 128 instructions, one block; the change itself made 192 of them. Rounds 2 and 3 of the first step took 5.0 and 4.6 us, so the sign "rounds of 5 us" nearly came, but not for the reason given with it: the quadrants do run together.

The steps, point by point. The additions: 0.40 forecast, 0.355 in a row. The first part: exponentials at 21.3 forecast, 23.0, 22.8 and 22.2 measured, mostly through the half clock behind PE's wait in round 1: with PE kept busy there they ended at 21.8. The wait was forecast, with 3.8 us (3.54). From there to the solution 13.4, 14.6 and 14.6 were forecast, 14.2, 16.3 and 14.8 measured. The last step shows the error bare: ACT's copy of round 1 begins 13.1 us after round 0, where it was expected at 13.5, and then the solution comes 19.4 later in place of 13.1, with 4.6 us of waits without a cause and no operands of DVE in between. It gained 1.0 in place of 6.8.

In the sum, an estimate: 20.4 at the full clock, less 9 to 12 for the supply of instructions (251.7, with the squarings of the changed kernel, and 254.1 against 242.3), less some 4 for the clock (6 forecast), is the 6.4 measured, within 2 us. The squarings with fewer instructions are 12 to 18 us below before, the forecast's 14.4 in the middle. But they also have shorter copies on ACT, and on two quadrants, without the crossing, they are already 8.8 below (251.6). So it isn't shown that the crossing alone would have brought the 14.4 without the supply's limit; its own share there is 9.3.

**The rivals.** The first, "the clock takes more", gave 10.5 us and 2964, and that number is near. Its reason is not: with the half level behind round 1's wait taken away, delta stayed at 254.5. The second and third did not come; the clock was at half for some 30 of 254 us, far from more than half of a step. The fourth, that the written-out layers bring nothing, is refuted by the stage and stays open by the whole time.

**The rule weighed.** Products with rows 0 to 63 and rows 64 to 127 write one bank at 16.5 ns an instruction over 127 of them, so the rule of Gotcha 1: PSUM Pressure (the Trainium skill, TensorEngine Tiling (Array Packing)) doesn't hold for outputs in different partitions, now in a long row too. The rule that did speak against the change stands elsewhere. The Trainium skill, Runtime: NRT & Kernel Launch, section Instruction fetch mechanics, says that an engine's instructions are refilled in blocks of 16 KiB, 256 instructions, while the ones before are executed; the 16.4 KB packets agree. It also says that this is hidden, since an engine issues more slowly than it is filled; with a weight load and a product in 16.5 ns PE does not.

## What to carry to other kernels

Count how long PE takes for 256 of its instructions, loads counted, as well as how long its columns take. Here 64-column products on four quadrants took 2.1 us for 256, a block came every 3.6 us, and the difference was lost unless a wait of another cause came before it. The cure here was wider products, not more parallel ones: letting two products share a left side was worth 11.8 us of delta, the crossing of quadrants 9.3. Where an engine's work halves but the order keeps the steps of a unit in series, move what the next unit needs ahead of what this one still waits for: that move gave 14.5 us in attention, more than the whole change. And before a stage is forecast from one profile, look at its mean clock: the same attention took 53.9 us at 0.87 and 50.0 at 0.93.

## What was not expected of the hardware

Where PE had run out of instructions, its waits ended 3.6 to 4.0 us apart, although a packet took only about 1.0 us of that, and the queue's share of the DMA engines is 0.3%. So most of the interval is not the transfer itself; what it is made of no run shows. The delta stage with the same code took 248.2 and 242.3 us at mean clocks of 0.92 and 0.96; if the clock is all of it, 5.9 us of a 250 us stage hang on how long it stays at half. With the scores of one more pair in PE's first wait, attention kept a mean clock of 1.00 instead of 0.93, worth 3.6 us by the two slow periods of the changed kernel.
